# Modulation of a diffusion step: every second weight tile as high and low parts, single-pass products, and a later load of the second weight block

## The reference

```python
def trunk_layer(x, mod, ...):
    shift, scale, gate = jnp.split(mod, 3, axis=-1)
    h = rmsnorm(x, p['norm_w']) * (1 + scale) + shift
    proj = h @ p['w_in']
    ...                              # gated DeltaNet branch and RG-LRU branch, merge
    return x + gate * mixed, ...

mod_ctx = (jax.nn.silu(c_ctx) @ w_mod[l] + b_mod[l])[None, None, :]
mod_lat = (jax.nn.silu(c) @ w_mod[l] + b_mod[l])[:, None, :]
```

## Time and profile before

| what | value |
|---|---|
| median of 3 runs | 1608.03 us (1605.88 to 1609.38) |
| profiled execution | 1610.26 us, its span 1608.5 us |
| PE busy | 1579.0 us, 98% |
| DVE busy | 1004.4 us, 62% |
| ACT busy | 802.7 us, 50% |
| POOL busy | 351.4 us, 22% |
| granted TensorE clock, mean | 0.995 |

### The profile page before, as it was taken

The page is one execution under the profiler, slowest core; times in us unless marked ns, Lnnn a source line. Parts: engine busy times, 40 slices in busy tenths (PEclk is TensorE's granted clock), DMA queues, the critical chain, the costliest instruction groups (busy, mean ns, idle before and its releaser), DMA issues. The chain is left out here.

```text
span 1608.5 us, 25106 instructions
## 1 busy us (share of the span) xinstructions
PE 1579.0 (98%) x9960; PEld 1505.0 (94%) x9960; DVE 1004.4 (62%) x1729; ACT 802.7 (50%) x1659; POOL 351.4 (22%) x273
## 2 busy tenths in 40 slices
PE   8999999999999999999998999999999999999997
PEld 3699999999999999999968999999999999999886
DVE  2679687796868779686835673574465641333444
ACT  5264565746567574655633766366446630311211
POOL 2132123221222322221210211221221122143110
PEclk9999999999999999999999999999999999999999
DMA  9221222120122212012240122122121261353123
GB/s 321 63 63 28 73 58 73 31 97 22 41 73 59 73 31 97 21 42 73 84 128 28 48 75 76 55 76 61 42 80 57 99 216 40 113 162 123 55 79 131
DMA packets 115999, 127.27 MB, mean 79 GB/s; under 512 B 6477, under 2 KB 97446, under 8 KB 115882
## 3 DMA queue, kind: packets, MB, share of 16 engines
q1 hardware_dynamic: 115594, 125.34, 24.5%
q10 hardware_dynamic: 288, 0.33, 0.1%
HBM read 105.56 MB, written 20.09 MB: 78 GB/s over the span
## 5 line engine op out<-in xcount | busy, mean ns | idle before, releaser
L124 PE MATMUL mb<-h_hi,w_hi 128*128 128x384 f32 x1088 | 364.1, 335 | 5.0 <-PEq L156 3.4
L125 PE MATMUL mb<-h_lo,w_hi 128*128 128x384 f32 x1088 | 363.5, 334 | 0.0
L126 PE MATMUL mb<-h_hi,w_lo 128*128 128x384 f32 x1088 | 363.5, 334 | 0.0
L124 PE MATMUL db<-h_hi,w_hi 128*128 128x384 f32 x808 | 285.6, 353 | 6.0 <-ACT d_row L554 2.8
L126 PE MATMUL db<-h_hi,w_lo 128*128 128x384 f32 x808 | 272.3, 337 | 0.0
L125 PE MATMUL db<-h_lo,w_hi 128*128 128x384 f32 x808 | 271.7, 336 | 0.0
L1708 POOL TENSOR_TENSOR w_lo<-w,w_hi 128x1024 fp32r<-128x1024 f32 x47 | 127.7, 2718 | 466.7 <-ACT w_hi L1738 466.7
L124 PEld LDWEIGHTS mb<-h_hi,w_hi 128*128 128x128 f32 x1088 | 204.2, 188 | 6.1 <-issue 3.6
L125 PEld LDWEIGHTS mb<-h_lo,w_hi 128*128 128x128 f32 x1088 | 204.2, 188 | 0.0
L126 PEld LDWEIGHTS mb<-h_hi,w_lo 128*128 128x128 f32 x1088 | 204.2, 188 | 0.0
L124 PEld LDWEIGHTS db<-h_hi,w_hi 128*128 128x128 f32 x808 | 153.1, 190 | 8.7 <-ACT padded_rows L554 2.7
(11 more groups left out here) (307 smaller groups left out, 2953.3 us busy)
## 6 DMA issues: line engine op xcount, KB each, us to landing
w<-in_w_in SPq DMA_DIRECT2D x48, 512.0 KB, 4.0
d_dt<-decay_rows SPq DMA_DIRECT2D x16, 576.0 KB, 5.5
d_qg<-decay_rows SPq DMA_DIRECT2D x16, 512.0 KB, 7.6
w<-in_w_gate SPq DMA_DIRECT2D x16, 512.0 KB, 4.1
branch_a<-d_kq SPq DMA_DIRECT2D x8, 576.0 KB, 3.2
branch_b<-l_z SPq DMA_DIRECT2D x8, 576.0 KB, 2.8
merge_gates_b<-l_gates SPq DMA_DIRECT2D x8, 576.0 KB, 5.3
m_in<-merge_gates_b SPq DMA_DIRECT2D x8, 576.0 KB, 3.8
```

The costliest lines, as they stand in the source:

```text
L124: pe.matmul(out, hi, rhi, start=(k == 0), stop=False)
L125: pe.matmul(out, hi, rlo, start=False, stop=False)
L126: return pe.matmul(out, lo, rhi, start=False, stop=(last and stop))
```

## The change

- The odd tiles (scale) are split: ScalarE copies tile 2t+1 to its high part (`mod_high`, into the still unused buffer of h's low parts), VectorE subtracts (`mod_low`) and writes the low part over the raw tile: `mod_lo0` and `mod_lo1` lie where `d_vt` and `d_cb` begin.
- silu(c) is split once (`silu_c_split`, four columns: high and low of both vectors). For an odd tile TensorE makes two products per half, four columns by the high part and four by the low part, in fp32r. Even tiles stay as they were.
- Banks 2 and 3 so hold four rows, the share of the high and of the low columns apart. The eight transposes of the scale half become products with `fold`, a 4 x 2 matrix that adds the rows by pairs.
- ScalarE gets one `mod_high` behind every second x tile, then, in order: mod_high(4), high(0), mod_high(5), the high part of the gate columns, mod_high(6), mod_high(7). VectorE gets `mod_low` ahead of the copies of x tiles 0, 2, 4, 6, 8, and three behind those of x tile 8.
- load(1) goes behind the last tile of the modulation. high(1) moves on ScalarE to the place behind the third high part of h.

```diff
             for t in range(KT):
                 mod_load(2 * t)
...
-                elif t == 6:
-                    load(1)
+            load(1)
             for dst, src in small:
...
+            act.wait_ge(S["silu_c"], 1)
+            act.activation(sch[:, 0:2, :], sc[:, :, :], ACT.Copy).then_inc(S["silu_c"], 1)
+
+            def mod_high(t):
+                n = 2 * t + 1
+                act.wait_ge(S[f"wm{n % NW}"], 16 * (n // NW + 1))
+                act.activation(mod_hi(t), wmod[n % NW], ACT.Copy).then_inc(S["wm_hi"], 1)
...
                 if t:
                     normalise(t - 1)
+                if t % 2:
+                    mod_high(t // 2)
             normalise(NT - 1)
+            mod_high(4)
             high(0)
+            mod_high(5)
             act.wait_ge(S["wg_in"], 16)
             act.activation(wghi[:, :, :], wg, ACT.Copy).then_inc(S["wg_hi"], 1)
-            high(1)
+            mod_high(6)
+            mod_high(7)
...
                 act.activation(R.hhi[:, k, :], hf[:, k % 2, :], ACT.Copy).then_inc(S["h_hi"], 1)
+                if k == 2:
+                    high(1)
...
+                n = 2 * t + 1
+                if t == 0:
+                    pe.wait_ge(S["silu_c"], 3)
+                pe.wait_ge(S["wm_lo"], t + 1)
+                for m in range(2):
+                    ms_ = slice(m * 512, (m + 1) * 512)
+                    pe.matmul(bank[2 + m][0:4, :], sch[:, :, t], mod_hi(t)[:, ms_], start=(t == 0), stop=False)
+                    mm = pe.matmul(bank[2 + m][0:4, :], sch[:, :, t], mod_lo(t)[:, ms_],
+                                   start=False, stop=(t == KT - 1))
+                mm.then_inc(S["mod_k"], 1)
...
-                mm = pe.transpose(bank[5][:, 2 * i:2 * i + 2], modrow[:, i * P:(i + 1) * P], R.ident[0:2, 0:2])
+                if i < KT:
+                    pe.transpose(bank[5][:, 2 * i:2 * i + 2], modrow[0:2, i * P:(i + 1) * P], R.ident[0:2, 0:2])
+                else:
+                    mm = pe.matmul(bank[5][:, 2 * i:2 * i + 2], modrow[:, i * P:(i + 1) * P], fold[0:4, :],
+                                   start=True, stop=True)
...
+            def mod_low(t):
+                raw = wmod[(2 * t + 1) % NW]
+                dve.wait_ge(S["wm_hi"], t + 1)
+                dve.tensor_tensor(mod_lo(t)[:, :], raw, mod_hi(t).bitcast(F32), ALU.subtract).then_inc(S["wm_lo"], 1)
+
             xt = R.xt
             for t in range(NT):
+                if t % 2 == 0:
+                    mod_low(t // 2)
                 dve.wait_ge(S["x_t"], t + 1)
...
                 ins.then_inc(S["x_e"], 1)
+            for t in range(5, KT):
+                mod_low(t)
             dve.wait_ge(S["rows_t"], 1)
```

More of the change, by code:

```diff
@@ L172, in front_stage @@
         row2 = sb("d_row2", [P, RAW])
+        with nc.sbuf_tensor("mod_lo1", [P, D], F32R) as mod_lo1:
+            pass
         cb_ = sb("d_cb", [P, CONV])
         kn = sb("d_kn", [P, NT, P])
+        with nc.sbuf_tensor("mod_lo0", [P, D], F32R) as mod_lo0:
+            pass
         vt = sb("d_vt", [P, NT, P])
@@ L202, in front_stage @@
         NL = len(wlast)
-        modrow = k2[0:2, :, :].rearrange("p a c -> p (a c)")
+        mod_lo = lambda t: (mod_lo0, mod_lo1)[t % 2]
+        mod_hi = lambda t: R.hlo[:, t, 0:D]
+        modrow = k2[0:4, :, :].rearrange("p a c -> p (a c)")
         crow = v2[0:2 * KT, 0:P]
         sc = sb("silu_c", [P, 2, KT])
+        sch = sb("silu_c_split", [P, 2 * 2, KT], F32R)
+        fold = sb("fold", [P, 2])
         sct = sb("silu_c_tanh", [P, 2 * KT])
@@ L892, in _ @@
             for t in range(KT):
[L893 to L898, removed]
+                n = 2 * t
+                pe.wait_ge(S[f"wm{n % NW}"], 16 * (n // NW + 1))
+                for m in range(2):
+                    mm = pe.matmul(bank[m][0:2, :], sc[:, :, t], wmod[n % NW][:, m * 512:(m + 1) * 512],
+                                   start=(t == 0), stop=(t == KT - 1))
+                mm.then_inc(S["mod_k"], 1)
[3 more added lines that the diff above has]
+                pe.wait_ge(S["wm_lo"], t + 1)
+                for m in range(2):
+                    ms_ = slice(m * 512, (m + 1) * 512)
+                    pe.matmul(bank[2 + m][0:4, :], sch[:, :, t], mod_hi(t)[:, ms_], start=(t == 0), stop=False)
+                    mm = pe.matmul(bank[2 + m][0:4, :], sch[:, :, t], mod_lo(t)[:, ms_],
+                                   start=False, stop=(t == KT - 1))
+                mm.then_inc(S["mod_k"], 1)
                 if t == 6:
@@ L1217, in low @@
                                   ALU.subtract).then_inc(S["w_lod"], 1)
+            dve.wait_ge(S["ident_in"], 16)
+            dve.tensor_tensor(fold[0:4, :], R.ident[0:4, 0:2], R.ident[0:4, 2:4], ALU.add)
             dve.wait_ge(S["c_t"], 1)
@@ L1226, in _ @@
                               ALU.mult).then_inc(S["silu_c"], 1)
+            dve.wait_ge(S["silu_c"], 2)
+            dve.tensor_tensor(sch[:, 2:4, :], sc[:, :, :], sch[:, 0:2, :].bitcast(F32), ALU.subtract).then_inc(S["silu_c"], 1)
+            def mod_low(t):
+                raw = wmod[(2 * t + 1) % NW]
+                dve.wait_ge(S["wm_hi"], t + 1)
+                dve.tensor_tensor(mod_lo(t)[:, :], raw, mod_hi(t).bitcast(F32), ALU.subtract).then_inc(S["wm_lo"], 1)
             xt = R.xt
             for t in range(NT):
+                if t % 2 == 0:
+                    mod_low(t // 2)
                 dve.wait_ge(S["x_t"], t + 1)
```

6 lines of the change are left out of this document (3 added, 3 removed).

## The result

| kernel | median of runs | profiled execution, its span | TensorE busy | mean granted clock of that execution |
|---|---|---|---|---|
| before | 1608.81 us (7 runs, 1605.88 to 1609.72) | 1610.26, 1608.5 us | 1579.0 us | 0.995 |
| after | 1616.00 us (7 runs, 1614.23 to 1619.20) | 1617.82, 1616.0 us | 1578.0 us | 0.992 |

The change makes the kernel slower: the ratio of after to before is 1.0045, with a 95% interval of 1.0035 to 1.0054, or +7.2 us. The prediction said +2.8 us and 1610.9 us; the median lies outside its range, on the slow side.

A forecast was written before the change was run, and what follows sets the result against it. The prediction took the modulation to be paced by VectorE's order and the last tile's landing and split, not by TensorE's work. +1.3 modulation, +0.2 VectorE's tail, +0.8 folds and +0.5 ports gave +2.8 us, a median of 1610.9, range 1605.5 to 1614.5.

The forecast's parts named there:

- What bounds the stage: Modulation: waits for low parts and landings outweigh 6.2 us of saved TensorE work; last product 49.9 for 48.6, +1.3 us.
- rival 2: Modulation: TensorE is the bound and the saved 6.2 us count, 1603.3, or 1605.8 with the last split exposed; chance 0.10.
- VectorE's tail: Behind the modulation: parameter copy, scalings and wg low part stand behind the last low part on VectorE, +0.2 us.
- The folds: Small pieces behind the modulation: eight transposes become fp32 products, 1.2 to 1.8 us for 0.6, +0.8 (+0.5 to +1.3).
- The ports: h loop: the second block's GpSimd low part and memsets collide with VectorE; TensorE idles 1.5 us for 1.04, +0.5.
- rival 1: h loop, VectorE's scaling for k=4: memsets follow at once and keep the port, +2.6 for +0.5, 1613.0; chance 0.33.
- The clock: Modulation, wait of 2.05 us at t=3: a rival had TensorE fall to half clock, costing 1.7 us, 1612.6; chance 0.07.

The follow-up runs named there:

- the kernel with the three costs away: The changed kernel with transposes for the fold products, filler products in the last tile's wait, and high(1) behind the last high part of h: 1609.94 us, 1.0008 of before.
- The move alone: The kernel before with only load(1) put behind the last modulation tile and high(1) behind the third high part of h: 1611.38 us, 1.0024 of before.
- the change with fillers: The changed kernel with ten filler products on TensorE ahead of its wait for the last tile's low part: 1612.89 us, 1.0033 of before.
- with transposes: The changed kernel with eight transposes of four rows for the fold products and one more small VectorE operation: 1611.98 us, 1.0019 of before.
- the kernel before with the longer wait: The kernel before, its last raw product waiting for a ScalarE copy of tile 15 and two VectorE subtracts: 1612.91 us, 1.0027 of before.
- high(1) last: high(1) moved behind the last high part of h: in the changed kernel 1612.02 us (1.0017 of before), in the kernel before 1.0002 and 0.9994.
- the pair of kernels with fillers: The changed kernel with filler products and high(1) behind the last high part of h: with folds 1612.18 us (1.0018), with transposes instead 1609.94 us (1.0008).

## Why the prediction was wrong

**What bounds the stage: right.** Waits for the low part in nearly every pair, split tiles of 0.92 us, VectorE's order and the landings as the pace. The size was too small, and near only by luck in the one profile. The last product was to end 1.3 us late, from an issue of tile 15 at 42.6 and a transfer of 3.8 us. It ended 0.7 late, from an issue at 41.06 and 4.9 us, as the pairs up to t=5 lost nothing: t=0 ended at 12.45 for the 13.0 worked out, the product of t=3 at 30.6 for 31.8. Over the eight profiles that split all odd tiles it ended at 49.4 to 52.1, on average 2.4 us later than in five profiles with the modulation of before (47.6 to 48.7); part of that is the last product itself at half clock in four of them. By the runs the split costs some 2.7 us at equal clock for the 1.3 + 0.2 of the sum. The split itself was worked out as 46.4 to 48.95, 2.55 us, and then called 2.45; it measured 2.3. The 6.2 us of saved work were rightly put at nothing, and rival 2 (TensorE is the bound after all, 1603.3) is refuted by the kernel with the three costs away, at 1609.9.

**VectorE's tail: near.** Its copies of the banks start at 49.47 for 48.72, 0.75 us late for 1.3 + 0.2 predicted in all, and no more than the product ahead of them was late: nothing was added.

**The folds: a term of the right kind, too small.** +0.8 was taken between +0.5 and +1.3; at full clock they cost +1.3 in the profile (1.92 us for 0.63) and +1.0 timed. A pass takes 0.12 us, as the filler's pass does in the earlier trace rows; a transpose's pass is no measure for it. I had both ends and chose the middle, where the fillers were the nearer kind.

**The ports: the mechanism right, the choice wrong.** The forecast took +0.5 and gave +2.6 to rival 1, with 0.33. The move alone costs 2.0 us of TensorE's idle time and 1.0024 in time. In the change it is 2.1 to 3.3 us by the pairs of kernels, of which some 0.9 was there before: 1.2 to 2.4 for the 0.5 of the sum. That VectorE's pending scaling would get in ahead of the memsets came true in neither profile of the change nor in the move alone. It came true in the change with fillers and with transposes, and in the kernel before with the longer wait: there the scaling got in behind the first memset (2.21 us), and the second memset waited for it (2.64 us for 2.02). An order that hangs on less than 0.1 us between two engines should have been given to the dearer outcome, or evenly.

**The clock: the step that failed.** The sum has no term for it. The prediction gave it 0.07, a price of 1.7 us, and looked for it at t=3, where the wait was 1.59 us and the clock held. Its argument against a fall was that a raw product stands before each wait and a split one behind. That looked at the wrong wait: it had itself worked out that tile 15 is split by 48.95, and before's tile 14 ends near 46.8, so a wait of up to 2.1 us with only small pieces behind it was in its own rows, and none was worked out for t=7. It measured 2.32 us, and the clock was at half from 49.5 to 59.7. By the traces the fall costs some 4 of the 6.1 us to the first projection: the folds and fillers take 1.6 and 2.15 us more than at full clock. In the timed runs the share is smaller: the mean clock is 0.0025 lower than that of before beside it, 2.7 us by the line above.

**The sum.** At equal clock the change costs +5.2 us. Put together from its parts it is 1.8 (split, less the idle time that high(1) last takes away) + 1.0 (folds, or 0.1 by the pair of kernels with fillers) + 2.1 to 3.3 (ports) = 4.0 to 6.1, and with 2.7 for the clock 6.7 to 8.8; measured were 7.2 and 8.4 us on the medians. The forecast had 1.5 + 0.8 + 0.5 and no clock. The parts don't add exactly: fillers that run late give VectorE a lead in the h loop and hide part of the ports' cost.

**Open.** How much of the clock's term belongs to the fall in the modulation and how much to later half-clock stretches. With the wait filled, the mean clock still is 0.0012 under before's, so the fillers give back about half of the 0.0025, some 1.4 us; with high(1) last they give back nothing that the runs can tell. The change has one more stretch at 73 us in both its profiles, behind the idle time of 1.76 and 2.55 us in the h loop; the profile with fillers has neither.

## What to carry to other kernels

When work is moved from an engine that looks busy to two others, list for each unit of it what the product then waits for. Here 6.2 us of saved passes met 9.8 us of waits. The last unit is the dearest, since nothing follows that could cover its split: keep it plain (+0.7 for +1.8 at equal clock here, within the noise of the two) or fill the wait. And a stage in which TensorE idles for a couple of microseconds should be priced at both clock levels, as one cannot tell from the idle time alone which it will get; the busy time won't show it, but unchanged fillers that take 5.09 us for 2.94 do.

## What the runs showed of the hardware

- The granted clock fell to half in a wait of 2.28 to 3.42 us ahead of the last product of the modulation, or up to 1.2 us behind it (six profiles of six), and with none of the waits of up to 1.78 us in the modulation. Elsewhere 1.76 us was followed by a fall, 3.05 us was not, and the same 2.03 us was in eight profiles of sixteen.
- Tiny fp32 products with 128 columns of weights take 0.12 us a pass, two passes each, at full clock (16 passes in 1.92 us), and 0.22 at half (3.55); transposes of the same size take 0.08 (8 in 0.63) with one pass.
- A GpSimd subtract of 128x1024 and a VectorE subtract of 128x1152 exclude each other: 3.66 us for 2.35, or 3.56 for 1.35. A VectorE operation that pends behind a GpSimd one may be held over two more GpSimd operations (scaling pairs of 6.74 and 7.18 us for 1.07), or get in behind the first of them (2.74 us, in three profiles).
